# The first matrix of two feed-forwards: two column tiles by seven half-width products of weight blocks and their sums, in place of eight

## What is computed

```python
x = layernorm(DEEPNORM_ALPHA * x + mix, ln1_g, ln1_b)

hid = jnp.square(jax.nn.relu(jnp.einsum('bsd,df->bsf', x, w_ff1)))   # w_ff1: 1024 x 4096
ff = jnp.einsum('bsf,fd->bsd', hid, w_ff2)                           # w_ff2: 4096 x 1024
return layernorm(DEEPNORM_ALPHA * x + ff, ln2_g, ln2_b)
```

## Time and profile before

| | |
|---|---|
| median of 3 runs | 2080.92 us (2080.81 to 2082.12) |
| the profiled execution, its own time | 2081.08 us |
| its span, first to last instruction | 2079.3 us |
| PE busy | 2052.4 us, 99% |
| PEld busy | 1692.3 us, 81% |
| DVE busy | 1097.8 us, 53% |
| ACT busy | 922.7 us, 44% |
| granted TensorE clock, mean | 0.998 of full |

### The profile page before, as it was taken

One profiled execution on the slowest core, in us unless ns is written; L12 is line 12 of the kernel. 1 busy time (PEld: TensorE's weight loads), 2 busy tenths in 40 slices (PEclk: granted clock), 3 DMA queues, 4 the chain that ended last, 5 costly groups with the idle time before them and its releaser, 6 DMA issues. The chain is left out here.

```text
span 2079.3 us, 24586 instructions
## 1 busy us (share of the span) xinstructions
PE 2052.4 (99%) x9744; PEld 1692.3 (81%) x9744; DVE 1097.8 (53%) x1794; ACT 922.7 (44%) x1502; POOL 150.5 (7%) x207
## 2 busy tenths in 40 slices
PE   9999999999999999999999999999999999999997
PEld 6888788888888888788688888888888788888886
DVE  6655566565343444477586333337677585333336
ACT  5664334334232322366357243344566357233243
POOL 0000000000000000354000000000353000000000
PEclk9999999999999999999999999999999999999999
DMA  7332222333333322633332333322632332332321
GB/s 241 99 105 62 81 66 97 124 100 122 103 100 102 102 81 62 183 109 90 116 102 82 101 102 101 102 81 62 178 102 81 117 102 88 109 99 90 101 81 41
DMA packets 201518, 211.37 MB, mean 102 GB/s; under 512 B 7803, under 2 KB 181115, under 8 KB 201404
## 3 DMA queue, kind: packets, MB, share of 16 engines
q1 hardware_dynamic: 194544, 194.13, 29.9%
q0 software_dynamic: 6352, 15.24, 2.8%
q10 hardware_dynamic: 508, 0.43, 0.1%
HBM read 194.55 MB, written 8.95 MB: 98 GB/s over the span
## 5 line engine op out<-in xcount | busy, mean ns | idle before, releaser
L619 PE MATMUL ps<-Phi,wh 128*128 128x512 f32 (+1 forms) x1200 | 475.9, 397 | 5.0 <-DVE x_fvv L1236 2.2
L622 PE MATMUL ps<-Phi,wl 128*128 128x512 f32 (+1 forms) x1200 | 455.2, 379 | 0.6 <-DVE wl L1153 0.6
L620 PE MATMUL ps<-Plo,wh 128*128 128x512 f32 (+1 forms) x1200 | 454.4, 379 | 0.0
L1153 DVE TENSOR_TENSOR wl<-stage,wh 128x1024 fp32r<-128x1024 f32 x249 | 303.5, 1224 | 69.9 <-ACT wh L1923 51.5
L1923 ACT ACTIVATE wh<-stage 128x1024 fp32r<-128x1024 f32 (+2 forms) x252 | 260.4, 1041 | 172.4 <-PE ps L622 157.5
L619 PEld LDWEIGHTS ps<-Phi,wh 128*128 128x128 f32 x1200 | 226.2, 189 | 55.2 <-issue 12.6
L622 PEld LDWEIGHTS ps<-Phi,wl 128*128 128x128 f32 x1200 | 225.6, 188 | 44.4 <-DVE wl L1153 1.0
L620 PEld LDWEIGHTS ps<-Plo,wh 128*128 128x128 f32 x1200 | 226.3, 189 | 40.6 <-issue 4.1
L619 PE MATMUL ps<-Qhi,wh 128*128 128x512 f32 (+1 forms) x680 | 256.6, 377 | 0.7 <-DVE Qlo L1169 0.7
L620 PE MATMUL ps<-Qlo,wh 128*128 128x512 f32 (+1 forms) x680 | 254.4, 374 | 0.0
L622 PE MATMUL ps<-Qhi,wl 128*128 128x512 f32 (+1 forms) x680 | 254.4, 374 | 0.0
(11 more groups left out here) (301 smaller groups left out, 2934.3 us busy)
## 6 DMA issues: line engine op xcount, KB each, us to landing
stage<-in_w_ff SPq DMA_DIRECT2D x64, 1024.0 KB, 5.3
stage<-in_w_in SPq DMA_DIRECT2D x39, 1024.0 KB, 5.3
stage<-in_w_up SPq DMA_DIRECT2D x16, 1024.0 KB, 5.4
stage<-in_w_down SPq DMA_DIRECT2D x16, 1024.0 KB, 5.2
stage<-in_w_in SPq DMA_DIRECT2D x30, 512.0 KB, 5.1
stage<-in_w_out SPq DMA_DIRECT2D x12, 1024.0 KB, 5.3
stage<-in_w_bg SPq DMA_DIRECT2D x4, 1024.0 KB, 5.2
vrev<-H SPq DMA_DIRECT2D x2, 2048.0 KB, 13.9
```

What stands on the lines that cost most here:

```text
L619: e.matmul(o, hi[:, k, cs_], hi_x[:, kx, tok], start=k == 0, stop=False)
L620: e.matmul(o, hi[:, k, cs_], lo_x[:, kx, tok], start=False, stop=False)
L622: t = e.matmul(o, lo[:, k, cs_], hi_x[:, kx, tok], start=False, stop=k == nk - 1)
L1153: t = e.tensor_tensor(lo, src, hi.bitcast(F32), ALU.subtract)
```

## The change

Groups 1 to 3 of the first matrix, in the feed-forwards F = 1 and F = 2, are computed in another way. Group 0 and the second matrix stay. Two up tiles (256 weight columns) are taken together as a 2 x 2 block product: the weights are cut into four blocks (two halves of the rows, two tiles of the columns), the input into four (two halves of the rows, two halves of the tokens). Eight half-width block products give the two tiles; seven products of blocks and block sums (Strassen's scheme in Winograd's form) give the same. The code calls this a `quad`; there are four in a group.

- **Products.** Q1, Q6, Q5, Q7, Q2, Q3, Q4, in this order, each 4 row blocks x 3 matmuls of 256 columns. Q2, Q3, Q4 are accumulated on the banks of Q1, Q5, Q7.
- **Weights.** The slab is the same 1 MB. It gives four pieces: the first column tile; two pieces of 1024 elements that are sums of blocks, made by `weight_sums` on VectorE with three additions of 1024, 512 and 512 elements; and half of the second tile (512 elements). Each piece is split by `high` and `low` as before. The sums are written where `lo` goes later.
- **Input.** Four sums of blocks of the input are made, split and kept, during the last four up tiles of group 0: on VectorE four additions and four low parts, on ScalarE four high parts, each of 1024 elements.
- **Combination.** In place of relu out of PSUM: ScalarE copies Q1 (`q1s`); VectorE makes U = Q1 - Q6, V = Q5 + U, c22 = Q7 - V, c12 = (Q5 + Q3) + U, c21 = (Q7 + Q4) - U, each of 256 columns; ScalarE does relu on c11, c12 and the second tile, and then the squares and high parts as before.
- **Waits.** On TensorE Q2 waits until Q1 is copied, Q3 until V is made, Q4 until c22 is made.

The diff, cut:

```diff
+PRODUCTS = (("Q1", 0, 0, 0), ("Q6", 2, 0, 1), ("Q5", 1, 4, 2), ("Q7", 1, 0, 3), ("Q2", 0, 4, 0), ("Q3", 2, 4, 2),
+            ("Q4", 3, 0, 3))
+
+ENDS = {"Q7": 1, "Q2": 0, "Q3": 2, "Q4": 3}
...
+            self.sums |= {len(self.pieces) + 1, len(self.pieces) + 2}
+            self.pieces += [(n, 0, cut) for cut in ((0, 8, 0, 128), (0, 8, 0, 128), (0, 8, 0, 128), (4, 8, 128, 256))]
...
+    def ready(self):
+
+        return self.prepared < len(self.weights.pieces) and len(self.ring) > (self.prepared in self.weights.sums)
+
     def prepare(self, apart=False):
...
+        if len(slots) == 2:
+            self.sums(*slots)
+        for slot in slots:
+            self.high(*slot)
 
         def rest():
-            if self.low:
-                self.low(i, u, freed)
+            for slot in slots:
+                self.low(*slot)
...
+    def quad(self, x, product, after):
+
+
+        i, base = self.used, 4 * (self.quads % 2)
+        self.used += 4
+        self.quads += 1
+        while self.prepared < i + 4:
+            self.prepare()
+        for name, piece, k0, b in PRODUCTS:
+            for k in range(4):
+                product(i, name, piece, base + b, k0, k)
+                self.tick()
+            after(i, name, base + b)
+            if name == "Q7":
+                while self.rest:
+                    self.rest.pop(0)()
+            if name in ENDS:
+                self.release(i + piece)
+                if name == "Q4":
+                    self.read_by[x] = i + 3
+                    if self.ready():
+                        self.rest.append(self.prepare(True))
+                else:
+                    self.prepare()
+        after(i, "end", base)
...
+                    again = {"Q2": act_x["q1", F, g, p], "Q3": vec_x["V", F, g, p], "Q4": vec_x["c22", F, g, p]}
+                    if k == 0:
+                        on.wait_ge(*([again[name]] if name in again else free[b]))
...
+            def weight_sums(second, third):
...
+                on.wait_ge(landed(i), *slot_over(freed), *slot_over(freed_v))
+                e.tensor_tensor(ws[u][:, :, :, :], one, other, ALU.add).then_inc(*w_low.up("sum", i))
+                on.wait_ge(w_low["sum", i])
+                e.tensor_tensor(ws[v][:, 0], ws[u][:, 1], a, ALU.add).then_inc(*w_low.up("sum of three", i))
+                on.wait_ge(w_low["sum of three", i])
+                e.tensor_tensor(ws[v][:, 1], ws[v][:, 0], b, ALU.add).then_inc(*w_low.up("sum", i + 1))
...
+                    if name == "Q7":
+                        on.wait_ge(gemm["product", i, name], vec_x["V", F, g, p])
+                        e.tensor_tensor(second, o, second, ALU.subtract).then_inc(*vec_x.up("c22", *key))
+                    if name == "Q3":
+                        before = (F, g, 2 * p - 2) if p else (F, g - 1, 6)
+                        on.wait_ge(gemm["product", i, name], act_x["square", *before])
+                        e.tensor_tensor(rl[0][:, 256:512], o, uu, ALU.add).then_inc(*vec_x.up("c12", *key))
+                    if name == "Q4":
+                        on.wait_ge(gemm["product", i, name])
+                        e.tensor_tensor(rl[1][:, 0:256], o, uu, ALU.subtract).then_inc(*vec_x.up("c21", *key))
+                    if name == "end":
+                        for j in (2 * p, 2 * p + 1):
+                            split_low(Qhi[:, j, :], Qlo[:, j, :], fq2[j % 2][:, :], act_x["hidden", F, g, j],
+                                      ("hidden", F, g, j))
...
+                if i in weights.sums:
+                    src = ws[u][:, :, :, :].rearrange("p j k c -> p (j k) c")
+                    on.wait_ge(w_low["sum", i], *slot_over(freed))
...
+                    if name == "Q1":
+                        on.wait_ge(gemm["product", i, name], *(
...
+                        e.activation(q1s, o, ACT.Copy).then_inc(*act_x.up("q1", *key))
...
+                    if name == "Q3":
+                        on.wait_ge(vec_x["c12", F, g, p])
+                        second = rl[0][:, 256:512]
+                        e.activation(second, second, ACT.Relu).then_inc(*act_x.up("relu", F, g, 2 * p))
+                        squared(0)
+                    if name == "Q4":
+                        on.wait_ge(vec_x["c21", F, g, p])
+                        e.activation(rl[1][:, :], rl[1][:, :], ACT.Relu).then_inc(*act_x.up("relu", F, g, 2 * p + 1))
+                        squared(1)
```

More of the change, by code:

```diff
@@ L49, in constants, with nothing @@
     return c
+def nothing(*args):
+    return None
 class Signal:
@@ L109, in __init__ @@
     def __init__(self, w_in, w_bm, w_bg, w_out, w_up, w_down, w_in2, w_out2, w_ff1, w_ff2):
-        self.slabs, self.pieces = [], []
+        self.slabs, self.pieces, self.sums = [], [], set()
         self.pair(w_in, 0)
@@ L191, with __init__ @@
 class Walk:
-    def __init__(self, weights, own, high=None, low=None):
+    def __init__(self, weights, own, high=nothing, low=nothing, sums=nothing):
         self.weights, self.own = weights, own
-        self.high, self.low = high, low
+        self.high, self.low, self.sums = high, low, sums
+        self.quads, self.rest = 0, []
         self.ring, self.slot, self.freed = [0, 1, 2, 3], {}, [None] * 7
@@ L226, in release @@
             self.ring.append(self.slot[i])
+    def ready(self):
+        return self.prepared < len(self.weights.pieces) and len(self.ring) > (self.prepared in self.weights.sums)
     def prepare(self, apart=False):
-        i = self.prepared
-        if i == len(self.weights.pieces) or not self.ring:
-            return None
[L232 to L236, removed]
+        if not self.ready():
+            return None
+        pieces = [self.prepared]
+        if pieces[0] in self.weights.sums:
+            pieces.append(pieces[0] + 1)
+        slots = []
+        for i in pieces:
+            self.prepared += 1
+            u = self.slot[i] = self.ring.pop(0)
+            slots.append((i, u, self.freed[u]))
+        if len(slots) == 2:
+            self.sums(*slots)
+        for slot in slots:
+            self.high(*slot)
         def rest():
-            if self.low:
-                self.low(i, u, freed)
+            for slot in slots:
+                self.low(*slot)
         if apart:
@@ L248, in piece @@
         most = max(self.prepared + 1 + (i + 1) % 2, i + 1) + more
-        while self.prepared < min(i + (ahead or self.ahead) + more, len(self.weights.pieces), most) and self.ring:
+        while self.rest:
+            self.rest.pop(0)()
+        while self.prepared < min(i + (ahead or self.ahead) + more, len(self.weights.pieces), most) and self.ready():
             self.prepare()
@@ L1160, in low @@
                 e.memset(both[:, :, m:32].bitcast(F32), 0.0).then_inc(*w_low.up(i))
-            w = Walk(weights, DVE, low=low)
+            def weight_sums(second, third):
+                (i, u, freed), (_, v, freed_v) = second, third
+                n = weights.pieces[i][0]
+                a, b = (stage[n % 2][:, 1024 * j:1024 * j + 1024].rearrange("p (k c) -> p k c", k=4)[:, :, 0:128]
+                        for j in range(2))
+                one, other = (bass.AP(tensor=stage[n % 2][:, :].tensor, offset=o, ap=[[2048, 128], [step, 2], [256, 4], [1, 128]])
+                              for o, step in ((0, 128), (128, 1024)))
+                on.wait_ge(landed(i), *slot_over(freed), *slot_over(freed_v))
[4 more added lines that the diff above has]
+                e.tensor_tensor(ws[v][:, 1], ws[v][:, 0], b, ALU.add).then_inc(*w_low.up("sum", i + 1))
+            w = Walk(weights, DVE, low=low, sums=weight_sums)
             h_over = [[] for _ in range(8)]
@@ L1516, in ff @@
                         w.gemm("P", 8, nothing, ev_up(F, g, j))
+                    if F and g == 0:
+                        w.finish()
+                    for p in range(4 if F and g else 0):
+                        w.quad("P", nothing, combined(F, g, p))
                     for j in range(whole if g == 3 else 8):
```

121 lines of the change are left out of this document (113 added, 8 removed).

## The result

| | before | after |
|---|---|---|
| median | 2080.91 us | 2166.1 us (2164.37 to 2166.34) |
| ratio | | 1.0406, 95% interval 1.0388 to 1.0424 |
| span of the profiled execution | 2079.3 us | 2164.4 us |

The kernel is 85.2 us slower. The forecast was 56 us slower, with a range up to 2163. The sign came out, and so did the chain in the quads; the size did not, because other losses stand beside it: two that Part 4 had put at nothing, and the clock, which was a rival.

What follows compares the result with a forecast made beforehand. TensorE was taken as the bound, but made to wait for VectorE and ScalarE inside the quads. Per group 12.55 us of stalls less 3.20 saved is 9.35 lost, six times 56 us: 2137 us, range 2103 to 2163.

Steps and rivals of the forecast that it cites:

- Part 4: Input sums in group 0, slab transfers and PSUM banks: all lie beside TensorE's work and cost nothing.
- Part 1: TensorE in the quads: 0.120 us a step, 10.08 us instead of 10.88 a quad, 3.2 us saved a group, 19.2 in all.
- Part 2: Instruction prices beside TensorE: per steady quad VectorE 9.4 us, ScalarE 8.1, each alone fitting 10.08 us of TensorE.
- Part 3: Alternating VectorE and ScalarE chain through a group: 12.55 us of stalls less 3.20 saved, 9.35 lost; 56 us over six groups.
- the turns: From `q1` to `q1`, quad 1 to 2 and quad 2 to 3: 11.52 and 13.22 us against 10.08 of TensorE.
- the tail to hidden block 6: Quad 3 to the first down tile: chain of 9.98 us against 8.40 of TensorE, a stall of 1.58 us.
- The stall of quad 2 that was forecast: TensorE waiting for `q1` at Q2 of quad 2: 1.44 us a group.
- Rival (c): Clock falls to half in the stalls: 13 us more, 2150; 2163 if in two stalls of a group; chance 0.13.
- Rival (a): Turn through both engines stays below 10.08 us, TensorE remains the bound: faster, 2061.7 or down to 2052 us; chance 0.08.

Runs made afterwards that it cites:

- e7: Changed kernel, same instructions reordered (low parts put off, pieces prepared ahead of Q1, Q6, Q2), input high parts two places later, banks 4 to 7 first: 2061.90 us.
- e5: Changed kernel plus 24 unused matmuls of 256 columns ahead of the wait at Q2 in quads 1 and 3: 2167.95 us.
- e1: Kernel before plus the input sums alone in group 0, read by nobody, without quads and weight sums: 2093.93 us.
- e2: Changed kernel with ScalarE's high parts of the input sums two places (about one tile) later, same instructions: 2152.64 us.
- e3: Changed kernel with the quads of a group beginning on PSUM banks 4 to 7 instead of 0 to 3: 2162.63 us.
- e9: e5 plus unused matmuls of 512 columns in each group's first down tile, ahead of the waits for hidden blocks 6 and 7: 2155.20 us.
- e10: Changed kernel with the low part of what is prepared behind Q3 put off until behind the next quad's c22, same instructions: 2181.76 us.
- e6: Changed kernel with what is prepared behind Q4 moved behind the next quad's Q1, so ScalarE copies Q1 first: 2145.46 us.

## Why the prediction was right and wrong

**Part 1 was right.** 0.120 us a step and 3.2 us a group: e7 gave 3.18, and 19.0 us in all against 19.2. The estimate by the step in "TensorE: Matmul & The Clock Gate" of the Trainium skill, Part 1, N / 2.4 GHz plus 2.5 ns, was 28 us; it was not reached.

**Part 2 was right in its prices.** Weight sums 1.22, 0.69 and 0.69 us, 256 elements 0.42. One link was mis-sized: U, V and c22 follow each other at 0.52 us from start to start (1208.97, 1209.49, 1210.02), where 0.45 was taken. With the handovers beside them that is 0.20 to 0.26 us in each of the three later turns of a group, 4.7 us over the six groups.

**Part 3 was right link by link.** In e5, where the clock was held in most quads, the turns are 11.72 and 13.46 us, forecast 11.52 and 13.22; the difference is that link. The changed kernel's own are 11.72 to 11.79 and 13.43. The first is 15.04 against 14.96, the tail to hidden block 6 10.24 against 9.98. The stall of quad 2 that was forecast can't be seen in the changed kernel, because PE at half rate came later than `q1` did; e5 showed it at 1.54. So the waits on `q1` are 7.9 us a group in two quads, where 9.5 in three were forecast.

**Part 4 failed, twice.** "Eight DVE instructions of 1024 (9 us) and four ACT ones in the last four tiles of group 0 lie beside 21.8 us of PE" was a sum of busy times, the very argument that Part 2 had just refused for the quads. The chain through group 0 was not followed. It costs 13.6 us by the trace; e1 showed 12.7 for it alone, and e2 gave back 13.5 by moving four instructions. And "The banks alternate by quad and are read long before" held for the quads among themselves, not for the first one of a group in F = 1, whose bank is that of the last down tile: 0.94 us three times, 2.8 us; e3 gave back 3.5, with a spread of several us.

**Rival (c) came true beside the forecast, and smaller than priced in the groups.** It was held at 0.13 and 13 us. The half rate was there behind both long stalls of each group, and by e9 it cost at least 6.2 us in the groups, plus 4.3 behind the stop in group 0, which the prediction didn't have (10.9 by the medians). "TensorE: Matmul & The Clock Gate" of the Trainium skill, "Why this matters for your kernels", names gaps between bursts as the cause. The changed kernel's trace agrees, as each of its fourteen stops of 3.0 us and more was followed by the half rate; e10 had stops of 3.33 us that were not. The prediction's "the stalls before (2.2 us at most)" misread rows 2, where 2.2 us is the sum of two waits and 1.3 the longer.

The sum then: 56.1 (forecast) + 13.6 (input sums, 4.3 of it clock) + 2.8 (banks) + 4.7 (the 0.52 us links) + 6.2 (clock in the groups) = 83.4; less 0.8 before and with 0.35 between the feed-forwards 83.0, measured 85.2. The 2.2 us that are left stand in e9's groups too, 1.3 of it in its last one, and were not traced. The terms are read from one execution of each kernel; where the half rate fell differed from group to group, by up to 1.6 us in the time. That the result came within 3 us of the range's end is no merit of the sum: 2163 was the price of the clock in two stalls, and most of the missing time lay elsewhere.

**Rival (a) fell, but for a narrower reason than it seemed.** Both engines do have room beside 10.08 us. The turn through both was a matter of order, not of work: e7 has it.

Left open: whether another order would allow the scheme in group 0 or in the first feed-forward too. It wasn't tried.

## What to carry to other kernels

When a change makes the bound engine wait inside its own tile for work of two others, add up the chain in program order, not busy times, and do so for every stretch that the change touches, the small preparatory one as well. An engine that works in a fixed order is idle wherever its next instruction waits; two engines that wait for each other in one tile take the sum of their shares, and setting one of them a tile back can remove all of that waiting at no cost. Before moving work out of an idle place, see who waits where it lands.

## What the runs showed of the hardware

- In the changed kernel all fourteen stops of TensorE of 3.0 to 5.1 us were followed by 7 to 26 matmuls at about twice the step (0.22 us for 256 columns, 0.43 for 512), 2.7 to 5.6 us in all, with a granted clock down to 0.50 in the rows. Stops of one length could differ: of six stops of 3.33 us in e10 three were followed by 14 to 26 such steps and three by none, of six of 2.49 us in e6 again three and three.
- Unused matmuls ahead of the wait cut these stops to 2.27 us and less. The half rate then followed in 3 of 12 cases in e5 and in 4 of 12 in e9, in place of 12 of 12.
- The matmul behind a stop takes 0.10 to 0.16 us more than a step before the next one starts (0.22 us to the next start at full clock, 0.38 at half, with 256 columns).
- Three VectorE instructions of 256 elements, each reading PSUM and the result before it, follow each other at 0.52 us; two that need nothing of each other at 0.33.
